# Decoder block with expert retrieval: where the gates' read stands in the load queue, ScalarE's order in the last expert tiles, and the gates' layout in memory

## The reference, cut to what matters

```python
def expert_block(args):
    hb, ib, gb = args
    u = jnp.take(u_tab, ib, axis=0)
    act = jax.nn.gelu(jnp.einsum('btd,bted->bte', hb, u), approximate=False)
    vv = jnp.take(v_tab, ib, axis=0)
    return jnp.einsum('bte,bted->btd', gb * act, vv)
```

## Time and profile before

| what | value |
|---|---|
| median of 3 runs | 2160.78 us (2153.29 to 2161.29) |
| profiled execution, its own time | 2160.44 us |
| profiled execution, span first to last instruction | 2158.2 us |
| mean granted TensorE clock | 0.924 of full |
| DMA | 432.00 MB, mean 200 GB/s over the span |
| expert stage | 1418.3 us to the end |

### The profile page before, as it was taken

How to read it: one execution, slowest core, us unless ns; L and a number is a source line. 1 busy time by engine, 2 the same in 40 slices (tenths; PEclk the granted TensorE clock), 3 DMA queues, 4 the chain that set the end, 5 groups by cost and what they waited for, 6 DMA issues and landing times. The chain is left out here.

```text
span 2158.2 us, 32371 instructions
## 1 busy us (share of the span) xinstructions
PE 1868.8 (87%) x11429; PEld 1631.1 (76%) x11429; DVE 1498.6 (69%) x2853; ACT 725.3 (34%) x1073; POOL 800.6 (37%) x451
## 2 busy tenths in 40 slices
PE   2988777879996998998988999879999889889897
PEld 1765466768875888998988999857777777778886
DVE  5999544452323578999988999856666666667677
ACT  3235322233325233332334444323333333332333
POOL 1443211113442337887872333222122222234342
PEclk8998877779998998999998999989999999999999
DMA  8751000012221227887876878868788878888885
GB/s 304 250 194 53 1 2 0 0 39 71 96 96 69 78 92 243 271 272 231 275 230 219 307 276 304 296 222 295 257 273 268 266 269 284 278 274 273 308 295 175
DMA packets 175491, 432.00 MB, mean 200 GB/s; under 512 B 15160, under 2 KB 91064, under 8 KB 173760
## 3 DMA queue, kind: packets, MB, share of 16 engines
q1 hardware_dynamic: 123008, 274.36, 36.6%
q0 software_dynamic: 36864, 134.23, 20.0%
q10 hardware_dynamic: 15552, 22.55, 2.8%
HBM read 383.38 MB, written 47.71 MB: 200 GB/s over the span
## 5 line engine op out<-in xcount | busy, mean ns | idle before, releaser
L1754 PE MATMUL bank<-v_hi,coef_hi 128*128 128x512 f32 x768 | 308.2, 401 | 62.7 <-DVE coef_lo L1829 62.7
L180 POOL DMA_INDIRECT own_rows<-in_peer_v_dram,own_row x128 | 200.5, 1567 | 436.3 <-DVE y_own L1844 417.5
L1754 PE MATMUL bank<-v_lo,coef_hi 128*128 128x512 f32 x768 | 305.9, 398 | 0.0
L1754 PE MATMUL bank<-v_hi,coef_lo 128*128 128x512 f32 x768 | 305.5, 398 | 0.0
L180 POOL DMA_INDIRECT own_rows<-in_u_rows_dram,own_row x128 | 194.4, 1519 | 299.2 <-DVE own_rows L1579 204.7
L1231 PE MATMUL bank<-h_hi,piece_hi 128*128 128x384 f32 (+1 forms) x672 | 241.1, 359 | 29.2 <-POOL piece_lo L1368 25.0
L1368 POOL TENSOR_TENSOR piece_lo<-piece,piece_hi 128x1024 fp32r<-128x1024 f32 x84 | 212.2, 2527 | 130.2 <-ACT piece_hi L1298 129.2
L1231 PE MATMUL bank<-h_lo,piece_hi 128*128 128x384 f32 (+1 forms) x672 | 236.6, 352 | 0.0
L1231 PE MATMUL bank<-h_hi,piece_lo 128*128 128x384 f32 (+1 forms) x672 | 236.3, 352 | 0.0
L1829 DVE TENSOR_TENSOR v_lo<-v_tile,v_hi 128x1024 fp32r<-128x1024 f32 x128 | 156.3, 1221 | 114.2 <-ACT v_hi L1789 114.2
L1754 PEld LDWEIGHTS bank<-v_hi,coef_hi 128*128 128x128 f32 x768 | 148.3, 193 | 102.2 <-issue 71.9
(11 more groups left out here) (341 smaller groups left out, 4132.5 us busy)
## 6 DMA issues: line engine op xcount, KB each, us to landing
v_tile<-in_peer_v_dram SPq DMA_DIRECT2D x128, 512.0 KB, 9.1
piece<-in_peer_u_dram SPq DMA_DIRECT2D x68, 512.0 KB, 4.4
ada<-in_w_ada_dram SPq DMA_DIRECT2D x48, 512.0 KB, 5.2
gate_scratch<-gate_block SPq DMA_DIRECT2D x12, 2048.0 KB, 7.6
gate_tiles<-gate_scratch SPq DMA_DIRECT2D x32, 768.0 KB, 7.2
gelu_scratch<-gelu_early ACTq DMA_DIRECT2D x104, 192.0 KB, 4.7
gelu<-gelu_scratch SPq DMA_DIRECT2D x104, 192.0 KB, 9.1
u_early<-in_peer_u_dram SPq DMA_DIRECT2D x36, 512.0 KB, 5.6
```

The costliest lines, as they stand in the source:

```text
L180: pool.indirect_dma_start(own_rows[:, n % R], None, tables[n // NS], bass.IndirectOffsetOnAxis(ap=own_row[:, n % NS:n % NS + 1], axis=0)). ...
L1754: last = nc.tensor.matmul(y_bank(t, half)[:], w[:, j, t * P:(t + 1) * P], x[:, j, c], start=(first and n == 0), stop=(final and n == 2))
```

## The change

The gates' read moves from a group's first tile (j == 0) to its last (j == G - 1), behind that tile's v load and gelu or u load; its wait keeps its value. `gate_scratch` is laid out by groups of four tiles, so that the read of a group is one run of 6 KB per partition (was 12 runs of 512 B), and the store of a slot is 32 runs of 512 B per partition (was one of 16 KB). ScalarE issues `v_hi` of tile e+1 after `coef_hi` of tile e, and, late, `u_hi` of tile e+2 directly after the Gelu of tile e.

```diff
@@ scatter_stage, SyncE
-                            sp.dma_start(spill[:, bass.ds(i * SLOTS + slot, 1)], block_g[:, slot:slot + 1]).then_inc(stored[slot], 16)
+                            sp.dma_start(spill[:, :, bass.ds(i * SLOTS + slot, 1)].rearrange("p g o j t -> p (g o) j t"), block_g[:, slot].rearrange("p (g j) t -> p g j t", j=4)).then_inc(stored[slot], 16)
@@ expert_stage, SyncE
-                sp.dma_start(gt[:, 0], spill[:, :, 0:G, :]).then_inc(s_g[0], 16)
+                sp.dma_start(gt[:, 0], spill[:, 0]).then_inc(s_g[0], 16)
-                    if j == 0 and i < GX - 1:
+                    if j == G - 1 and i < GX - 1:
                         if i:
                             sp.wait_ge(coef_ready, i * G)
-                        sp.dma_start(gt[:, (i + 1) % 2], spill[:, :, (i + 1) * G:(i + 2) * G, :]).then_inc(s_g[(i + 1) % 2], 16)
+                        sp.dma_start(gt[:, (i + 1) % 2], spill[:, i + 1]).then_inc(s_g[(i + 1) % 2], 16)
@@ expert_stage, ScalarE
+                split_v(0)
                 for e in range(NX):
                     if e == OWN_GELU:
                         act.wait_ge(row_used, NS)
                         nc.scalar.activation(own_coef[:], own_act[:], ACT.Gelu).then_inc(own_gelu, 1)
-                    if NE <= e + 1 < NX:
-                        split_u(e + 1)
-                    split_v(e)
                     if e >= NE:
                         act.wait_ge(u_done, e - NE + 1)
                         nc.scalar.activation(gel[:, e % G, :], bank[e % 2][:, 0:TD], ACT.Gelu).then_inc(gelu_ready, 1)
+                    if NE <= e + 2 < NX:
+                        split_u(e + 2)
                     split_c(e)
+                    if e + 1 < NX:
+                        split_v(e + 1)
@@
-SPILL = (P, TD // TB, P, TB)
+SPILL = (P, EXP_TILES // 4, TD // TB, 4, TB)
```

## The result

| | median | range | runs |
|---|---|---|---|
| before | 2160.85 us | 2153.29 to 2161.29 | 4 |
| changed | 2098.73 us | 2088.18 to 2103.37 | 4 |

The ratio is 0.9714, with a 95% interval of 0.9669 to 0.9758: 62 us faster. The profiled execution of the changed kernel took 2088.18 us, the fastest of its four, so the sum over its stages comes out some 10 us larger than the difference of the medians.

What follows compares the result with a forecast made beforehand. TensorE and VectorE were taken to bound the scatter stage, TensorE with its waits the expert stage. From 2160.4 us: -83 read's move, 0 ScalarE's order, -1 layout's reads, +21 its stores, -63 in all: 2097 us, range 2072 to 2132.

Steps and rivals of the forecast that it cites:

- The read's move: Expert stage: gates' read at the last tile removes TensorE's waits and low clock, 89 us, less 6 for transfers: -83 us.
- the unblocked stretch: Last group of the expert stage, 2085 to 2115 us, with no gates' read to issue; TensorE busy 30.00 of 30 us.
- The 6 us: Expert stage: allowance for transfers needing 318 GB/s early and 339 late, where 322 was seen; takes 89 us to 83.
- The cause of the stall: Expert stage, SyncE's queue: the gates' read waits for `coef` and holds back the v load, or late the u load.
- ScalarE's order: Expert stage: early nothing changes, late the u load's landing is hidden, and splits leaving the Gelu's front win nothing: net 0.
- the bound of 1 us a tile: Late expert tiles: if the u load comes later, `coef_hi` and VectorE wait, at most 1 us in each of 24 tiles.
- The layout, read side: Gates' reads in 6 KB runs instead of 512 B: hidden except the first, which VectorE awaits at the start: -1 us.
- The layout, store side: Scatter stage: 12 stores in 512 B runs, each 2.5 us longer, delay VectorE's next load: 25.6 us, taken as +21.
- the forecast's own formula: Scatter stage: 8 stores pass on their whole added length, 4 pass on what exceeds 1.08 us of slack.
- The transfers kept up: Rival, expert stage: transfers don't keep up, at 308 GB/s 29 us less is won, 2126 us; chance 0.18.
- The slow stores: Rival, scatter stage: each store 6 us longer (13.6 us), costing 68 us instead of 21, total 2144 us; chance 0.10.
- the turn to a loss: Rival, scatter stage: stores 7.4 us longer, landing in 15 us, use up the gain of 84 us; chance of slower 0.05.

Runs made afterwards that it cites:

- e5: Kernel before, with the wait for `coef` left in the group's first tile and only the gates' read moved to the last: 2060.79 us, ratio 0.9515.
- e11: Kernel before, gates' read in place, a third gates buffer so that its wait is for a group earlier: 2066.43 us, ratio 0.9545.
- e4: Kernel before, with the gates' read moved and ScalarE's new order, layout as before: 2063.60 us, ratio 0.9528.
- e1: Kernel before, with only the gates' read moved from the group's first tile to its last: 2060.25 us, ratio 0.9513.
- e3: Kernel before, with only ScalarE's new order: 2175.40 us, ratio 1.0055.
- e2: Kernel before, with only the layout by groups (512 B store runs, 6 KB read runs): 2153.94 us, ratio 0.9956.
- e7: Changed kernel, with each store issued behind the next unit's `u_early` load instead of ahead of it: 2052.88 us, ratio 0.9493.
- e8: Kernel before, with the gates' read moved to the last tile and stores behind the next unit's load, 16 KB store runs: 2051.22 us, ratio 0.9485.
- e12: Same kernel as e8, measured again on another occasion: 2047.90 us, ratio 0.9475.
- e10: Same kernel as e7, measured again beside e8 on the same chip: 2056.59 us, ratio 0.9503.
- e6: Changed kernel, with memory laid out by groups of 8 tiles (1 KB store runs, 512 B read runs): 2088.10 us, ratio 0.9660.

## Why the prediction was right, and where its steps were off

2097 us was forecast and 2098.73 measured. The two mechanisms were right, the loads freed in the expert stage and the stores' price in the scatter stage, but that the sum is within 2 us is luck.

- *The read's move*, -83. Measured -95.3 in the stretch. All 89 us of stall and lost clock that I had counted went, and some more: the clock is 1.00 throughout, where the unblocked stretch had 0.97 behind a wait. The 6 us that I left for transfers that can't quite keep up were not needed: 323 and 327 GB/s with a DMA share of 0.88 to 0.92.
- *The cause of the stall.* "It is held back by a wait that it doesn't need" is half of it. With the wait alone (e5) the load is early enough for TensorE in the early tiles (ScalarE still waits some 1 us for it), and with the read alone (e11) too. The load was late by the stop and by 768 KB ahead of it; the last group, which I read as the change tried once, had neither, and so could not tell the two apart. (A small misreading: the v load waits for `v_lo` of tile 4i-3 and the read for `coef` of tile 4i-1, which is two tiles and not three.)
- *ScalarE's order*, 0. Right with the move (e4 against e1). Alone it costs 0.55% (e3): the bound of 1 us a tile in the range was for this mechanism, but I had not seen that the order is a loss where the u load is late.
- *The layout, read side*, -1. Right in the changed kernel. The forecast called the reads hidden; in the kernel before they were not, and there the layout alone wins 39 us of stretch (e2).
- *The layout, store side*, +21. The step that was mis-sized: I took a store 2.5 us longer, and it is 3.9 (11.5 against 7.6), above even the 3.3 of the nearest row. By the forecast's own formula that makes 8 x 3.9 + 4 x 2.8 = 42 us; the scatter stage grew by 30.1 in the two profiles, and by 39 against e4. The waits were also shared out otherwise: the four that had 1.08 us of slack came to 3.6 us on average (formula: 2.8), the other seven grew by 2.1 each (formula: 3.9). The forecast had the load wait for a longer store; the trace shows it held at its own issue for 5 to 6 us, a term that the sum doesn't have. How this and the longer landing share the price is open. That a store's place ahead of the load is the cause is shown by e7. By the rule of the Trainium skill, "DMA: Bandwidth & Descriptors" (Why small descriptors are slow), about 3 cycles for each packet, the estimate is a store 1.1 us longer; the trace differs, 3.9.
- Two errors cancelled: 12 us more were won in the stretch and 9 more lost in the scatter stage. The two profiles' stages sum to -66 where -63 was forecast; the medians differ by 62.

Of the rivals none came. The transfers kept up. The slow stores (6 us longer) and the turn to a loss (7.4 us) were not reached. The forecast's own terms for the layout, -1 and +21, say that it loses; that it could be left out was not concluded from them. e1 shows it: it keeps all of the gain.

## What to carry to other kernels

A transfer with a wait of its own, in a queue that serves more urgent loads, should stand where its wait is already over; moving one read behind three more tiles' loads won 100 us here, and moving the store behind one load another 9 to 12 us with its 16 KB runs (e8, e12 against e1), or 42 to 46 with runs of 512 B (e10, e7 against the changed kernel; medians of different occasions). When a stall has two ingredients, take each away alone before naming one as the cause. When a layout is changed to help a read, count what the write pays and who is queued behind the write.

## What the runs showed of the hardware that was not expected

- Behind a store in 512 B runs, SyncE's queue is itself held up while it issues the next load. With 1 KB runs (e6) the issue of such a `u_early` load takes 1.7 to 2.4 us, and with 16 KB runs 0.33 to 0.43. Issue times of the `u_early` loads, minimum, median and maximum in ns, changed kernel:

```profile
L1656 SPq DMA_DIRECT2D u_early<-in_peer_u_dram x34: 328/919/5930, 1134.3 to 1410.2; - x34
```

and of the stores:

```profile
L1660 SPq DMA_DIRECT2D gate_scratch<-gate_block x12: 557/563/678, 1156.6 to 1432.0; - x12
```

In the kernel before the same loads took 328 to 449 ns to issue.
- From 1536 runs up, the issue time of a transfer doesn't go by their number here: 563 ns for a store in 4096 runs of 512 B, 564 for one in 2048 runs of 1 KB (e6), 550 for a read in 1536 runs, and 355 for a store in 128.
- TensorE ran at a granted clock of 1.00 through 460 us of windows of unbroken products in e1, while the transfers moved 323 to 326 GB/s. The kernel before, with waits of 0.6 to 4.6 us in most groups, had 0.96 and 0.94.
